# Double gates in the second layer, a new order of transfers, and filler products in the tails of both SSM projections

## The reference

```
m_x = adaln(c, ada_w[i], ada_b[i])                     # six modulation vectors of a layer
hx  = rms_norm(x, n_pre) * (1 + mods_x[1]) + mods_x[0]
proj = concatenate([hc, hx]) @ w_in                    # rq rk rv rg | sz sxbc sdt | aq ak av | bgate
u = silu(short_conv(sxbc) + b)                         # 3 taps; channels: 1024 of x, 256 of B, 256 of C
ssm: y = chunked state-space recurrence of u, dt; y = head_rms(y * silu(z)) * norm_w
br = einsum('bnw,nwd->bnd', branch outputs, w_branch)
merged = sum(sigmoid(bgate) * br);  y = merged @ w_out
```

## Time and profile before

| | us |
|---|---|
| median of three runs | 2928.18 |
| the profiled execution | 2928.81 |
| its span, first to last instruction | 2927.5 |
| PE busy | 2643.0 (90%) |
| DVE busy | 1451.9 (50%) |
| ACT busy | 1299.6 (44%) |
| POOL busy | 761.5 (26%) |

### The profile page before, as it was taken

The page is one execution under the profiler, slowest core; times in us unless marked ns, Lnnn a source line. Parts: engine busy times, 40 slices in busy tenths (PEclk is TensorE's granted clock), DMA queues, the critical chain, the costliest instruction groups (busy, mean ns, idle before and its releaser), DMA issues. The chain is left out here.

```text
span 2927.5 us, 34992 instructions
## 1 busy us (share of the span) xinstructions
PE 2643.0 (90%) x13281; PEld 2145.9 (73%) x13281; DVE 1451.9 (50%) x1709; ACT 1299.6 (44%) x1677; POOL 761.5 (26%) x346
## 2 busy tenths in 40 slices
PE   6887999999898899998968898888699999999997
PEld 4664778977777678877755687656588888888886
DVE  2465412431442323201455315342588888888886
ACT  2461432242342322213542423334477777677765
POOL 0321244243213244433322633624100000000000
...
DMA packets 234571, 496.55 MB, mean 170 GB/s; under 512 B 14864, under 2 KB 111408, under 8 KB 234288
## 3 DMA queue, kind: packets, MB, share of 16 engines
...
## 5 line engine op out<-in xcount | busy, mean ns | idle before, releaser
L290 POOL TENSOR_TENSOR unit_lo<-raw_units,unit_hi 128x1024 fp32r<-128x1024 f32 x244 | 588.5, 2433 | 1171.2 <-ACT unit_hi L282 1171.2
L2555 DVE TENSOR_TENSOR moe_unit_lo<-moe_raw,moe_unit_hi 128x2048 fp32r<-128x2048 f32 (+1 forms) x283 | 612.0, 2175 | 103.6 <-ACT moe_unit_hi L2549 100.7
L2549 ACT ACTIVATE moe_unit_hi<-moe_raw 128x2048 fp32r<-128x2048 f32 (+1 forms) x280 | 509.1, 1821 | 219.0 <-PE bank L311 217.8
L282 ACT ACTIVATE unit_hi<-raw_units 128x1024 fp32r<-128x1024 f32 x246 | 246.6, 1052 | 525.6 <-PE bank L311 427.6
L309 PE MATMUL bank<-unit_hi,hT_hi 128*128 128x256 f32 (+1 forms) x1168 | 422.9, 362 | 36.2 <-PEq L1289 13.7
L310 PE MATMUL bank<-unit_lo,hT_hi 128*128 128x256 f32 (+1 forms) x1168 | 402.0, 344 | 0.0
L311 PE MATMUL bank<-unit_hi,hT_lo 128*128 128x256 f32 (+1 forms) x1168 | 401.5, 344 | 0.0
L309 PE MATMUL bank<-moe_unit_hi,xe_T_hi 128*128 128x512 f32 (+1 forms) x768 | 290.4, 378 | 1.1 <-DVE xe_T_lo L2586 1.1
L309 PEld LDWEIGHTS bank<-unit_hi,hT_hi 128*128 128x128 f32 x1168 | 228.0, 195 | 84.5 <-issue 49.4
L310 PE MATMUL bank<-moe_unit_lo,xe_T_hi 128*128 128x512 f32 (+1 forms) x768 | 287.1, 374 | 0.0
L311 PE MATMUL bank<-moe_unit_hi,xe_T_lo 128*128 128x512 f32 (+1 forms) x768 | 286.3, 373 | 0.0
...
## 6 DMA issues: line engine op xcount, KB each, us to landing
moe_raw<-in_moe_w SPq DMA_DIRECT2D x224, 1024.0 KB, 7.4
...
ada_unit<-in_ada_w SPq DMA_DIRECT2D x40, 1024.0 KB, 5.3
...
ada_first<-in_ada_w SPq DMA_DIRECT2D x8, 1024.0 KB, 13.6
...
```

The lines of the kernel that those rows point to most:

```text
L282: act.activation(half_of(view(whi, g), half), half_of(view(raw, g), half), ACT.Copy).then_inc(hi_ready, 1)
L290: eng.tensor_tensor(lo, whole, hi.bitcast(F32), ALU.subtract).then_inc(lo_ready, 1)
L2549: act.activation(moe_hi[:, at_unit % RING, 0:n], moe_raw[:, at_unit % SLOTS, 0:n], ACT.Copy).then_inc(hi_m, 1)
L2555: dve.tensor_tensor(moe_lo[:, at_unit % SLOTS, 0:n], moe_raw[:, at_unit % SLOTS, 0:n], moe_hi[:, at_unit % RING, 0:n].bitcast(F32), ALU.su ...
```

## The change

The list of its parts:

- `ssm_project`: in the last unit the group m is now the outer loop. After each group ACT, DVE and PE carry its channels on while PE multiplies the next; the turns of channels 4 to 9 stand between the groups, in banks 5 and 0 (6 stays free for filler). In layer 1 the two C groups are computed for tiles 2 and 3 only (`first_segment`), in both units of the block.
- Z_TAIL = 0.7: three half pieces of filler in layer 0 (two in layer 1) stand behind the last group; four (two) at the head of `ssm_mix`, 25 (12) behind.
- `ssm_mix`, SP: in each slot the modulation weights are issued first, and the filler's unit two slots later than before.
- `ada_finish` moves from the end of `ssm_mix` to the start of `ssm_gate`.
- Layer 1: both halves of a gate are projected in `ssm_gate` and `ret_gate`, and `merge` has branch products alone (banks 4 to 7), for two of the three branches.
- `ret_project`: the last unit goes tile by tile (`project_last`), with K's turns between the tiles.
- `att_project`: the last unit goes tile by tile in the order 2, 3, 0, 1, and DVE takes each tile as it is complete.

```diff
@@ -224,17 +224,17 @@
             def add_merge(n):
 
                 for b in range(2):
-                    if b:
+                    if b and l == 0:
                         add_gate(n, b)
...
             stage_units(f"ssm{l}", add_ssm)
             stage_units(f"zf{l}", lambda: add_fill(COL["sz"]))
-            stage_units(f"z{l}", lambda: add_gate(1, 0))
+            stage_units(f"z{l}", lambda: [add_gate(1, b) for b in range(l + 1)])
             stage_units(f"merge1_{l}", lambda: add_merge(1))
             stage_units(f"ret{l}", lambda: [cols_of("rq", 1), cols_of("rk", 1), cols_of("rv", 2)])
             stage_units(f"rf{l}", lambda: add_fill(COL["rg"]))
-            stage_units(f"g{l}", lambda: add_gate(0, 0))
+            stage_units(f"g{l}", lambda: [add_gate(0, b) for b in range(l + 1)])
...
@@ -410,7 +410,10 @@
                 for k in range(4):
                     a = [h[:, 4 + k, tile * P:(tile + 1) * P] for h in src]
                     last = three(pe, ps[banks[j]][:, :], a, [w[0][:, k, :], w[1][:, k, :]], False, k == 3)
-                last.then_inc(unit_used if j == len(tiles) - 1 else tile_done, 1)
+                if j == len(tiles) - 1:
+                    last.then_inc(unit_used, 1)
+                else:
+                    tile_done(last, j)
...
             conv_banks = [[0, 1, 2, 3], [4, 5, 6, 0], [1, 2, 3, 4]]
+            turn_banks = [5, 0]
+
+            def first_segment(n, m):
+
+                return l if n == 2 and m >= 2 else 0
...
+                    def tap(act, n, m):
+                        i = 4 * n + m
+                        lo = 256 * first_segment(n, m)
+                        act.activation(acc[:, m, lo:], ps[conv_banks[n][m]][:, lo:], ACT.Identity,
+                                       scale=cw[:, 12 + i:13 + i], bias=cb[:, i:i + 1]).then_inc(acc_set, 1)
+
+                    def channels(act, n, m):
+                        i = 4 * n + m
+                        act.wait_ge(conv_done, i + 1)
+                        lo = 256 * first_segment(n, m)
+                        act.activation(u_of(i)[:, lo:], acc[:, m, lo:], ACT.Silu).then_inc(u_ready, 1)
...
                         split_hi(act, a1 + 2 * n + 2)
+                        if n == 2:
+                            for m in range(5):
+                                if m < 3:
+                                    act.wait_ge(group_done, m + 1)
+                                elif m == 3:
+                                    act.wait_ge(unit_used, b0)
+                                if m < 4:
+                                    tap(act, n, m)
+                                if m:
+                                    channels(act, n, m - 1)
+                            for slot in range(6):
+                                fill.act(act, slot)
+                            continue
...
@@ -802,9 +829,10 @@
                     dve_step(dve, dve.tensor_tensor(wst[:, :], wst[:, :], dtv[:, :], ALU.mult))
                     for i in range(4):
                         take_turned(i)
-                    conv(2)
-                    for i in range(4, 10):
-                        take_turned(i)
+                    for m, now in enumerate(((4, 5), (6, 7), (8,), (9,))):
+                        conv(2, [m])
+                        for i in now:
+                            take_turned(i)
...
                             g = a1 + 2 * n + u
                             pe.wait_ge(lo_ready, 2 * (g + 1))
                             wh, wl = view(whi, g), view(wlo, g)
+
+                            def product(k, m):
+                                a = [wh[:, k, m * P:(m + 1) * P], wl[:, k, m * P:(m + 1) * P]]
+                                kk, lo = 4 * u + k, 256 * first_segment(n, m)
+                                return three(pe, ps[conv_banks[n][m]][:, lo:], a, [h[:, kk, lo:] for h in hT], kk == 0, kk == KD - 1)
+
+                            if n == 2 and u == 1:
+                                for m, now in enumerate(((4, 5), (6, 7), (8,), (9,))):
+                                    for k in range(4):
+                                        last = product(k, m)
+                                    last.then_inc(group_done if m < 3 else unit_used, 1)
+                                    if m == 3:
+                                        pe.wait_ge(conv_done, 11)
+                                        for slot in range(6):
+                                            fill.pe(pe, slot)
+                                    for i in now:
+                                        turn(i)
+                                continue
...
-        Z_TAIL, Z_HEAD = [0, 0], [6, 6]
+        Z_TAIL, Z_HEAD = [0.7, 0.7], [6, 6]
...
-                    for slot in range(slots):
-                        fill.load(sp, 7 + slot)
+                    for slot in range(slots + 2):
                         for i in ada_in_slot(slot):
                             if i + 2 < len(ada_units):
                                 load_ada(sp, i + 2)
+                        if slot >= 2:
+                            fill.load(sp, 5 + slot)
...
-                    dve.wait_ge(ada_turned, n_chunks)
-                    for i, (la, c) in enumerate(ada_chunks):
-                        ada_finish(dve, la, c, ada_cols(i), by_half=True)
...
+            def finish_modulation(dve):
+                for i, (la, c) in enumerate(ada_chunks):
+                    ada_finish(dve, la, c, ada_cols(i), by_half=True)
+
+            return finish_modulation
...
+        def gate_products(pe, l, a0, tiles):
+
+            n = len(tiles)
+            for b in range(l + 1):
+                project(pe, a0 + 2 * b, range(n * b, n * b + n), tiles)
...
-                        if g == 0:
-                            split_hi(act, a0 + 1)
+                        if g <= l:
+                            split_hi(act, a0 + g + 1)
...
-                    split_hi(act, a0 + 2)
+                    for g in range(a0 + l + 2, b0 + 1):
+                        split_hi(act, g)
...
                 @block.vector
                 def _(dve):
+                    finish_modulation(dve)
...
-                    project(pe, a0, range(n), tiles)
+                    gate_products(pe, l, a0, tiles)
                     turn_to_outT(pe, y, tiles, range(KD), lambda f: (scaled, f // 4 + 1), turned, parts, LATE_BANKS)
...
+            both = l == 1 and not whole
+            m0 = a0
...
-                    for b in range(0 if whole else 2):
+                    for b in range(2 if both else 0):
+                        for j in range(n):
+                            act.activation(gate[:, b, j, :], ps[n * b + j][:, :], ACT.Sigmoid).then_inc(gate_out, 1)
+                        for g in range(m0 + 2 * b + 2, m0 + 2 * b + 4):
+                            split_hi(act, g)
+                    for b in range(0 if whole or both else 2):
...
+                            branch_sum = ps[4 + j + (n * b if both else 0)][:, :]
                             if first:
-                                dve.tensor_tensor(out, gate[:, b, j, :], ps[4 + j][:, :], ALU.mult).then_inc(merged_out, 1)
+                                dve.tensor_tensor(out, gate[:, b, j, :], branch_sum, ALU.mult).then_inc(merged_out, 1)
...
+                    for b in range(2 if both else 0):
+                        project(pe, m0 + 2 * b, range(4 + n * b, 4 + n * b + n), tiles, outT)
+                    for b in range(0 if whole or both else 2):
...
+                                if n == 3 and j < NT - 1:
+                                    act.wait_ge(tile_done, j + 1)
+                                elif n == 3:
+                                    take_turned(act, [RH + j])
+                                    act.wait_ge(unit_used, b0)
                                 act.activation(v[:, tile, (n - 2) * 512:(n - 1) * 512], ps[banks[n][j]][:, :],
                                                ACT.Copy).then_inc(out, 1)
-                    take_turned(act, range(RH, 2 * RH))
+                                if n == 3 and j < NT - 1:
+                                    take_turned(act, [RH + j])
...
+                    def k_turns(last, j):
+                        last.then_inc(tile_done, 1)
+                        turn(RH + j)
+                        if j == NT - 2:
+                            turn(RH + j + 1)
+
                     for n in range(4):
                         if n >= 2:
                             pe.wait_ge(out, done[n - 2])
                         for u in range(2):
-                            project_half(pe, a0 + 2 * n, u, banks[n], blocks[n])
+                            if n == 3 and u == 1:
+                                project_last(pe, a0 + 2 * n, banks[n], blocks[n], hT, k_turns)
+                            else:
...
-                    for i in range(RH, 2 * RH):
-                        turn(i)
...
-                    split_hi(act, a0 + 2)
```

(15 more changed lines are left out.)

64 lines of the change are left out of this document (27 added, 37 removed).

## The result

The kernel after takes 2851.59 us (median of four runs, 2847.75 to 2854.07), the kernel before in the same session 2926.57 us (2923.68 to 2935.05). The ratio is 0.9738, 95% interval 0.9714 to 0.9762: 75 us faster, where 60.3 were forecast. The profiled execution took 2853.09 us against 2928.81, 75.7 us less.

What follows compares the result with a forecast made beforehand. PE, busy for 90% of the span, was taken as the bound, through its idle times and lower clock. 2.3 + 7.9 + 3.6 + 17.5 + 8.0 + 4.0 + 5.0 + 3.0 + 9.0 = 60.3 us off 2928.8 gave 2868; range 2853 to 2886.

Steps and rivals of the forecast that it cites:

- Part 1: Layer 0's SSM projection tail and mix head: stage end 0.3 us earlier, DVE chain 2.0 us shorter; 2.3 us gained.
- Part 2: Layer 1's SSM projection tail and mix head: mix begins 5.4 us earlier, DVE chain 2.5 us shorter; 7.9 us gained.
- Part 3: Fewer half pieces of filler in the mix slots, 25 for 27 in layer 0 and 12 for 13 in layer 1; 3.6 us.
- Part 4: Transfers in both mixes: waits for modulation weights and slow clock behind them go, less late units; 17.5 and 8.0 us.
- the charge: In both mixes, modulation units sharing time with a z unit come 1 to 3 us late; 5 and 4 us charged.
- rival (b): Mixes: no late weights (+9) and the clock high over the whole mix (+4); time 2855 us, chance 0.13.
- Part 5: `ada_finish` moved from mix end into the gate stage: 2.4 us in layer 0, 1.6 in layer 1; 4.0 us.
- Part 7: Tails of retention's projections (1.5 us in each layer, 3.0) and attention's projections (9.0 us).
- Part 6: Layer 1's double gates: SSM pair ends about 4 us earlier, retention pair 1 us; 5.0 us.
- (a): Mixes: DMA too slow for two slots, Part 4 mostly becomes many small waits; 2884 us, chance 0.20 with (d).
- (c): Mixes: PE waits for z units delayed behind modulation weights, transfers cost 90 us; 2984 us, chance 0.03.
- (d): Stage ends: the order has no effect, POOL and DVE late everywhere; 2887 us, chance 0.20 together with (a).

Runs made afterwards that it cites:

- experiment 4: Kernel after with no filler in the projections' tails (Z_TAIL 0 in both layers): 2847.13 us, ratio 0.9723.
- experiment 12: Kernel after with layer 1's C groups computed for all four tiles: 2859.55 us, ratio 0.9755.
- experiment 1: Kernel after with SyncE's old order of transfers in both mixes (weight unit first, modulation weights behind it): 2881.55 us, ratio 0.984.
- experiment 2: Kernel before with nothing but SyncE's new order of transfers in both mixes: 2896.54 us, ratio 0.9895.
- Experiment 3: Kernel after with one modulation unit in every slot from the first on, in place of one in 1.4 slots (1.6 in layer 1): 2874.53 us, ratio 0.9819.
- experiment 6: Kernel after with DVE's last step of the modulation back at the end of the mix: 2853.20 us, ratio 0.9746.
- experiment 7: Kernel after with single gates in layer 1, merge projecting the second half again: 2857.47 us, ratio 0.9754.
- experiment 5: Kernel after with the projections of retention and attention ending as before (all products, then copies and turns): 2874.86 us, ratio 0.9812.
- experiment 8: Kernel after with the SSM projection as before (k outer in last unit, Z_TAIL 0, full C groups, turns in banks 5 and 6): 2862.73 us, ratio 0.9775.

## Why the prediction was wrong in size, point by point

**Parts 1 and 2 (2.3 and 7.9; 1.5 and 7.8).** Right. POOL's split ends the stage, PE stands idle for 5.8 us behind the last turn, and the long `cum_lhs` and `cum_row` are gone. I had argued that taking half pieces into the tail gives nearly nothing back at the stage's end in layer 0; experiment 4 shows that in layer 1 it loses 3.3 us. In layer 1 most of the gain is the C groups, 4.8 us up to the first slot and 6.7 with the mix (experiment 12).

**Part 3 (3.6).** The half pieces were counted right (25 and 12), what they are worth was not measured by itself, and where POOL's last split falls was not asked. In the kernel before it met DVE's state updates so that PE waited 4.49 us and then ran at half clock for some us; with filler in the tail the meeting comes earlier and PE waits 0.92 us. Less the 1.72 us at another update, the waits alone are 1.7 us shorter. This was in no term, nor was the wait of 4.49 us at 1460.64 in layer 1 on the other side.

**Part 4 (25.5; by the order alone 30 to 33).** This is the step that failed. I charged 9 us because "two slots are some 7 us" and a landing beside a z unit takes 7.6. But a unit does not come in each slot: layer 0 has 24 in 33 slots, so unit i+2 has 10.0 us in the mean, not 7, and a landing of 8.1 us is in time. One wait of 0.83 us was left. Without the charge Part 4 is 34.5 us, and the order alone was worth 32.7 and 33.5 in the stages of experiments 1 and 2: of the 9 us only 1 to 2 were due. Experiment 3 makes my assumption true, one unit in a slot, and then the late units are there: 6.7 and 10.2 us of waits, 23 us in the end. So late units of this kind exist, and the condition for them was not met here. I also read medians as if they held for each: of the five units in the earlier trace rows that "landed in 5.2 us each" one took 7.08, and of the three with 7.6 one took 9.97. Without the charge the sum would have been 69.3 us and the time 2859.5. This is rival (b), which had 0.13; it is the nearest of the cases. Its words on the clock were right for layer 0 from 190 us on (1.00), not for the whole mix (0.75 and 0.90 between 160 and 190 us).

**Part 5 (4.0; 4.4 and 1.6).** The two steps came out. This is the second step that failed, together with Part 7: the prediction put the slow running behind a wait at nothing wherever it falls into the next stage. That the gate stage of layer 0 then begins at the higher clock, 1.6 us, was missing; experiment 6 brings the 30.5 us back.

**Part 6 (5.0; 5.4 from the traces, 7.6 undone).** Right in size: the wait before the turns went from 3.14 us to 0.52. Of the waits "before units 3 and 4" one of 0.78 us before the fourth is there; the one of 1.34 us before the second exists with single gates too (1.37 in experiment 7). The turns came 27.8 us behind the stage's start for 25.6. Nearly 3 of the 7.6 us are slower running, which the part had only for the row itself.

**Part 7 (3.0 and 9.0; 2.6 and 11.2).** Retention right, as far as one profile tells with 3 us of scatter in layer 0. For the attention I counted the wait and the turns at the high clock, and not that the next stage also starts slowly behind a wait of 5 us. That is 4.3 us in the two mixes between before and after and 4.4 us in experiment 5, and 2.2 us more in the projections, of which 1.0 are the turns (0.88 us spared in each layer, where the part counted 0.8 in all) and 1.2 stay open.

**Sum of what was missing.** Of the 15.4 us between 60.3 and 75.7, the SSM mixes have 6.7 (7 to 8 us of the charge that were not due, and smaller things on both sides, among them the meeting and the wait at 1460.64, which I did not separate), the gate stage behind the mix and the attention's mixes 1.6 + 4.3, the attention's projections 2.2, and stages with unchanged code 2.8 + 0.3, which is luck; less 1.65 at the start and 0.9 in Parts 1, 2, 6 and 7's first half. Rivals (a), (c) and (d) fell: of many small waits for modulation weights one of 0.83 us appeared, PE waited for no z unit in either mix, and the stage ends moved (experiments 7, 8 and 12). By the charge alone the prediction missed some 7.5 us and would have stayed in its range; it took the slow stretches and the luck as well.

What stays open: which restart runs at the higher clock when code and idle time are the same. The idle time of 2.24 us before retention's gate is the same in all kernels, and the stage behind it takes 28.5 or 30.0 us.
